# Bidirectional encoder layer on Trainium2: how the first RMSNorm gets its weight row at the beginning

## What is computed

```python
x = x + 0.5 * swiglu(rmsnorm(x, norm_ffn1), w_gate, w_up, w_down)      # D_FF = 2816
x = x + hybrid_mixer(rmsnorm(x, norm_mix), ...)                        # windowed attention and gated linear attention
x = x + 0.5 * swiglu(rmsnorm(x, norm_ffn2), ...)
y = rmsnorm(x, norm_final)

def rmsnorm(x, gain):
    return x * rsqrt(mean(x * x, axis=-1) + EPS) * gain
```

## Time and profile before

| | |
|---|---|
| median of three runs | 2169.91 us (2168.96 to 2171.39) |
| profiled execution, from first to last instruction | 2169.4 us; no time around it is given, the runs' median is 0.5 us longer |
| TensorE matmuls busy | 2138.6 us (99%) |
| VectorE busy | 1499.5 us (69%) |
| ScalarE busy | 842.6 us (39%) |
| GpSimd busy | 330.1 us (15%) |
| mean granted TensorE clock | 0.998 |
| the loads of x and of the weight row at the beginning, from issue to landing | 3.9 to 9.4 us, median 7.0 us |

### The profile page before, as it was taken

One profiled execution on the slowest core, in us unless ns is written; L12 is line 12 of the kernel. 1 busy time (PEld: TensorE's weight loads), 2 busy tenths in 40 slices (PEclk: granted clock), 3 DMA queues, 4 the chain that ended last, 5 costly groups with the idle time before them and its releaser, 6 DMA issues.

```text
span 2169.4 us, 32769 instructions
## 1 busy us (share of the span) xinstructions
PE 2138.6 (99%) x11956; PEld 1921.3 (89%) x11956; DVE 1499.5 (69%) x2704; ACT 842.6 (39%) x1688; POOL 330.1 (15%) x324
## 2 busy tenths in 40 slices
PE   6999999999999999999999999999999999999998
PEld 6999999999988888888888888899999999988887
DVE  7766677676666686988754556777777667757676
ACT  7333222222343355755543334422323322333343
POOL 7111111111100002201002344211111111100000
PEclk9999999999999999999999999999999999999999
DMA  4322222332586566433355972222322222387554
GB/s 128 101 82 91 92 88 88 97 101 97 176 292 211 174 208 171 126 111 94 94 149 170 292 229 101 65 94 92 115 82 82 92 91 88 113 291 257 174 186 166
DMA packets 245987, 301.17 MB, mean 139 GB/s; under 512 B 24194, under 2 KB 159746, under 8 KB 245828
## 3 DMA queue, kind: packets, MB, share of 16 engines
q1 hardware_dynamic: 237188, 285.97, 41.2%
q10 hardware_dynamic: 8640, 13.11, 1.7%
HBM read 206.29 MB, written 88.47 MB: 136 GB/s over the span
## 4 chain that ended last, share of the span: by engine, by line
PE 95%; DVE 2%; POOL 1%; DMA 1%; issue 1%; ACT 1%; SPq 0%; ACTq 0%; POOLq 0%; DVEq 0%
PE ps L2485 16%; PE ps L2481 12%; PE ps L2483 10%; PE ps L2484 10%; PE ps L2493 8%; PE ps L2495 8%; PE ps L2494 8%; PE ps L2408 4%; PE ps L2410 4%; PE ps L2409 4%; PE ps L2426 2%; PE ps L2428 2%; PE ps L2427 2%; PE ps L2680 1%; PE ps L2654 1%; POOL hs L1121 1%
## 5 line engine op out<-in xcount | busy, mean ns | idle before, releaser
L2485 PE MATMUL ps<-hs,w_lo 128*128 128x384 f32 (+1 forms) x992 | 305.0, 307 | 0.0
L2493 PE MATMUL ps<-w_hi,dh 128*128 128x512 f32 x770 | 300.2, 390 | 0.0
L2495 PE MATMUL ps<-w_hi,dh 128*128 128x512 f32 x770 | 299.7, 389 | 0.0
L1959 DVE TENSOR_TENSOR dh<-dr,dh 128x640 fp32r<-128x640 f32 x154 | 127.2, 826 | 161.4 <-ACT dh L1357 161.2
L2494 PE MATMUL ps<-w_lo,dh 128*128 128x512 f32 x610 | 237.3, 389 | 0.0
L2483 PE MATMUL ps<-hs,w_hi 128*128 128x384 f32 (+1 forms) x644 | 214.4, 333 | 3.4 <-DVE hs L1802 2.6
L1357 ACT CAST dh<-dr 128x640 fp32r<-128x640 f32 x154 | 112.2, 729 | 269.9 <-PE ps L2495 250.1
L2484 PE MATMUL ps<-hs,w_hi 128*128 128x384 f32 (+1 forms) x644 | 213.9, 332 | 0.0
L2481 PE MATMUL ps<-hs,w_hi 128*128 128x512 f32 x588 | 210.2, 391 | 0.0
L2481 PE MATMUL ps<-hs_first,w_hi 128*128 128x512 f32 x588 | 210.2, 391 | 0.0
L2484 PE MATMUL ps<-hq,w_hi 128*128 128x384 f32 x616 | 205.8, 334 | 0.0
(11 more groups left out here) (321 smaller groups left out, 4826.2 us busy)
## 6 DMA issues: line engine op xcount, KB each, us to landing
dr<-hid_mid SPq DMA_DIRECT2D x154, 320.0 KB, 3.2
w_raw<-in_w_ffn_down SPq DMA_DIRECT2D x176, 256.0 KB, 3.6
hid_mid<-st SPq DMA_DIRECT2D x88, 320.0 KB, 4.3
w_raw<-in_w_ffn_gate SPq DMA_DIRECT2D x44, 512.0 KB, 4.1
w_raw<-in_w_ffn_up SPq DMA_DIRECT2D x44, 512.0 KB, 3.9
hid_mid<-sg SPq DMA_DIRECT2D x66, 320.0 KB, 2.2
hq<-o_mid SPq DMA_DIRECT2D x70, 128.0 KB, 3.6
w_raw<-in_w_in SPq DMA_DIRECT2D x14, 512.0 KB, 5.4
```

Source lines behind the costliest of these rows:

```text
L1959: v.tensor_tensor(a_lo, DR[f][n % D_HID][:, :], a_hi.bitcast(F32), ALU.subtract).then_inc(W["a_lo"], 1)
L2485: last = mm(out, lo[:, k, :], b_hi, start=False, stop=k == 3, skip_group_check=True)
L2493: mm(out, hi, w_h, start=first and p in D_FRESH, stop=False, skip_group_check=True)
L2495: return mm(out, lo, w_h, start=False, stop=last, skip_group_check=True)
```

## The change

The weight row's load and the identity's leave SP's queue. ScalarE's queue issues both at its very beginning, ahead of the first square, and the weight row is now written to all 128 partitions of `gain_first` by one DMA (512 KB written). The two spreading matmuls, their wait and their mark are gone; VectorE waits for `gain_loaded` and reads the row from SBUF.

```diff
@@ -353,8 +353,6 @@
         def x_first(t):
             return piece(*X_SLOT[t])
 
-        GAIN_BANK = 2
-
         def xs_first(n):
             return piece(4, 3 + n % 4)
 
@@ -465,7 +463,7 @@
         gain_loaded = sem("gain_loaded")
         expo_set = sem("expo_set")
         pe_marks = sem("pe_marks")
-        GAIN_SPREAD, OUT_EARLY = 1, 2
+        OUT_EARLY = 1
 
         def named(prefix, names):
             return {k: sem(f"{prefix}_{k}") for k in names.split()}
@@ -742,9 +740,7 @@
                 sp.dma_start(to, g.to_broadcast([P, D_MODEL])).then_inc(gain_loaded, 16)
 
             load_x(0)
-            sp.dma_start(gain_first[0:1, :, :], norm_ffn1.rearrange("a (h n) -> a h n", h=2)).then_inc(gain_loaded, 16)
             load_x(5)
-            sp.dma_start(ident[:, :], c_ident).then_inc(ident_loaded, 16)
             load_x(1)
             load_x(6)
             load_gu(0, 0)
@@ -1396,6 +1392,8 @@
                         elif s + D_LEAD + 1 >= G_STEPS:
                             d_hi(f, s + D_LEAD + 1 - G_STEPS)
 
+            act.dma_start(gain_first, norm_ffn1.rearrange("a (h n) -> a h n", h=2).to_broadcast([P, 2, HALF])).then_inc(gain_loaded, 16)
+            act.dma_start(ident[:, :], c_ident).then_inc(ident_loaded, 16)
             norm_squares(0, 0)
             norm_squares(0, 1)
             for i in range(HT):
@@ -1776,10 +1774,10 @@
                     dve.wait_ge(x_spilled[n % 2], 16 * (HT + n // 2 + 1))
                     gain = gain2[:, :].rearrange("p (h n) -> p h n", h=2)
                 else:
-                    dve.wait_ge(pe_marks, GAIN_SPREAD)
+                    dve.wait_ge(gain_loaded, 16)
                     if n >= 4:
                         dve.wait_ge(N["turned"], 4 * (n // 2 - 1))
-                    gain = ps[:, GAIN_BANK:GAIN_BANK + 2, :]
+                    gain = gain_first
                 v.scalar_tensor_tensor(out=xs_norm(f, n), in0=x_norm(f, t), scalar=rstd[:, 2 * f, t:t + 1], in1=gain,
                                        op0=ALU.mult, op1=ALU.mult).then_inc(N["scaled"], 1)
 
@@ -2535,11 +2533,6 @@
                 last.then_inc(W["tile"], 1)
 
             pe.wait_ge(const_set, ONES)
-            pe.wait_ge(gain_loaded, 16)
-            for half in range(2):
-                last = mm(ps[:, GAIN_BANK + half, :], ones[0:1, 0:1].to_broadcast([1, P]), gain_first[0:1, half, :],
-                          start=True, stop=True)
-            last.then_inc(pe_marks, 1)
             pe.wait_ge(ident_loaded, 16)
             for i in range(3):
                 norm_turn(0, i)
```

## The result

The changed kernel takes 2176.82 us (median of seven runs, 2176.54 to 2177.32) against 2169.85 us of the kernel before, timed beside it (seven runs): 7.0 us longer, ratio 1.0032, 95% interval 1.0022 to 1.0042. The profiled execution spans 2175.5 us, 6.1 us more than that of before.

A forecast was written before the change was run, and what follows sets the result against it. The start was taken as the bound: a chain over loads of x, VectorE and GpSimd before TensorE's dense work. 1.1 + 1.2 + 1.8 + 0.1 + 0.3 = +4.5 us on 2169.91 gave 2174.4 us, range 2170.6 to 2177.6.

The forecast's parts named there:

- my case: Main forecast: SBUF operand makes VectorE and GpSimd exclude each other at the start; +4.5 us, own range +2.9 to +6.0.
- rival 2: Whole holds: six meetings each cost a whole operation, landing moves 1.35 us in full; +6.5 us, 2176.4 us; chance 0.16.
- The landing: Loads of x at the start: broadcast's extra bytes make the sixth tile land later, +0.65 us, lower end -1.35.
- Scalings 1 to 4: First norm's start: second and third scalings hold back GpSimd's ssq and roots, first block at 15.1 us; +1.1 us.
- The pair at 18.34: Scalings before the second block: second's ssq and root wait, one subtraction slips in ahead; +1.2 us.
- The pair at 26.56: Scalings running into four subtractions: one ahead of the second scaling, another ahead of the low part, 0.9 us each; +1.8 us.
- The last pair and the clock: Pair at 37.16, behind the products' start, covered by VectorE's idle time, +0.1 us; TensorE's lower clock level, +0.3 us.
- The signs: Expected in the trace: first product at 38 to 39 us, sixth tile's square 17.4 to 18.7, four subtractions near 6 us.
- Rival 1: Not slower: exclusion falls beside the path at the start, only the landing is left, +0.65 us, 2170.6 us; chance 0.15.
- Rival 3: A late broadcast: landing after 10.2 us, each further microsecond paid again; at 12 us +6.3, 2176.2 us; chance 0.04.

The follow-up runs named there:

- experiment 10: Kernel before with only the queue changed: ScalarE issues the 4 KB row and identity, TensorE still spreads the row; 2168.91 us, second set 2168.86 us.
- Experiment 1: Kernel before with the changed kernel's loads (512 KB broadcast and identity on ScalarE's queue), row still spread by TensorE and read from PSUM; 2169.47 us, ratio 0.9998.
- Experiment 2: Kernel before with the changed kernel's loads and TensorE's spread kept; first four scalings read the row from SBUF, other six from PSUM; 2172.21 us, ratio 1.0010.
- experiment 5: Kernel before plus ScalarE's copy of the spread row into SBUF, read there only by the seventh and eighth scaling; 2173.76 us, ratio 1.0017.
- experiment 8: Kernel before with the changed kernel's loads, TensorE's spread kept; all scalings read SBUF except seventh and eighth, which read PSUM; 2174.16 us, ratio 1.0020.
- experiment 9: Kernel before with the changed kernel's loads, TensorE's spread kept; all scalings read SBUF except ninth and tenth, which read PSUM; 2175.21 us, ratio 1.0026.
- experiment 6: Kernel before plus ScalarE's copy of the spread row into SBUF, read there only by the ninth and tenth scaling; 2171.96 us, ratio 1.0009.

## Why the prediction was right, and where it was not

The direction and the mechanism held: 2176.82 us lies in the range (2170.6 to 2177.6), above the 2174.4 us forecast and above my case's own range, which ended at +6.0 us. That it lies in the range is in part luck: the upper end came from rival 2, and neither its six meetings at the whole price nor its landing in full are what happened. By its steps, with block 0, 1, 2 and the product as marks:

- **The landing, +0.65 us.** Wrong by its size. The sixth tile landed where it had (17.33 us), for the queues moved 340 GB/s from 2 to 10 us; before it was 284. Half of the difference comes with the earlier issues alone (312 GB/s in experiment 10's second set, where the sixth tile's square starts at 16.95 us): by these traces, what the issues gave, some 0.4 us, the broadcast took. What I had not worked out is the first tile: its square starts at 6.92 to 6.95 us in every trace with the broadcast and at 4.43 to 4.64 without. That the two share the bandwidth is my reading. Experiment 1 shows that by itself this costs nothing that can be measured.

```profile
2.00:10.00 8.00, 0.00 (x0) 0.00 (x0) 0.87 (x1) 3.64 (x6) 1.21 (x3) 1.00 1.01 340
```

- **Scalings 1 to 4, +1.1 us; measured +3.3.** This is the term that failed. I let the second scaling start at its old time and counted two delayed roots. With the first tile late, the first scaling ran from 9.13 us and held the second tile's ssq (0.93 us) as well, so that all three roots waited: a chain of scaling, ssq, root of 2.01 us a turn, 3 x 2.01 = 6.0 us from the first scaling to the fourth, where before it was 4.4. And the fourth met GpSimd's sum of weights at 15.08 us (2.28 for 1.28 us), an operation that I had not put in its way. The later first scaling is 0.7 of the 3.3 us, the chain 1.6 and that meeting 1.0. Experiment 2: +2.7 us in the time. No kernel has these scalings from SBUF and the first tile at its old time, so how much of the chain goes back to the late tile is not shown.
- **The pair at 18.34, +1.2 us; measured +0.9** at block 1, by another road: since VectorE was later, both roots were ready, and the pair met one subtraction, the low part another.
- **The pair at 26.56, +1.8 us; measured +1.0.** I counted two new meetings and kept the two old ones, five operations against four subtractions of which one had already run. The two new ones are right, at 2.05 us together (experiments 5 and 8); what I had missed is that VectorE, being late, is spared one of the others (1.1 us).
- **The last pair and the clock, +0.1 and +0.3 us; measured +0.9** from the product to the end (2135.9 us after, 2135.0 before), of which 0.4 by the end of the last transposes. The sum is near and its parts are not. In the last pair the cover failed: it took 4.32 us, made TensorE wait 1.42 us and costs 1.6 to 2.25 us by the medians (experiments 9 and 6). My cover, VectorE's idle 1.30 us at 40.92, was a wait for TensorE at its lower clock level; the two traces of experiment 10 show that without that stretch there is none. The clock gave the difference back in the profiled executions: the 16 transposes behind the first product took 1.91 us where they had taken 2.97. The low level had fallen ahead of the products (0.50 from 28.0 to 34.3 us, full behind it), where TensorE had time to spare. I had taken the stretch in the products as paid already; it is paid in the one profiled execution, and most timed runs of the kernel before are of the shorter group. Against experiment 1, which has no such stretch either, it is 2.7 us from the product to the end (2135.9 for 2133.2).
- **The signs.** The first product at 39.60 us came behind the 38 to 39 that I had named, the sixth tile's square at 17.33 a little ahead of the 17.4 to 18.7. Four subtractions took up to 7.5 us and not 6. The first three scalings kept their 1.28 us, since beside the tiny ssq it is GpSimd that waits; the longer ones are the fourth and one in each of the next two pairs.

Rival 1 (only the landing, +0.65) is refuted: the fourth scaling and all three pairs took longer, and experiment 1 has the landing at nothing. Rival 3 (a late broadcast) too: it landed in 4.7 us, at 5.4 us. Rival 2 had the price of a meeting nearer than I: 1.0 to 1.1 us on VectorE, where I had taken 0.9. The Trainium skill, SBUF — State Buffer, section SBUF: two separate sides, has the lock held for the whole instruction; the ssq that ends 0.06 us behind a scaling of 1.28 us agrees with that. Rival 2's other half, the landing in full, did not show: the sixth tile came no later than before, and 0.4 to 0.7 us later than in experiment 10. The Trainium skill, DMA: Bandwidth & Descriptors, section Issuing engines are not separate DMA queues, gives a second issuer the sequencer's time back and no more. That the landing must then move by the whole 1.35 us was my conclusion, and it left out the gaps that earlier issues and the broadcast fill.

## What to carry to other kernels

Where VectorE and GpSimd both work on the critical path, look at which of VectorE's operands lie in SBUF: an operation with one of its two in PSUM runs beside GpSimd, the same one with both in SBUF takes turns with it, about 1 us per meeting here for both engines. Two matmuls that put a row into PSUM can thus be cheaper than a transfer that is free. Count meetings by walking both instruction lists in time, tiny operations included, since a chain that goes back and forth between the engines pays in each turn. An engine that comes later meets others, or none, so the costs of single edits need not add; and before medians that differ by 1 or 2 us are compared, look where the low clock fell.

## What the runs showed of the hardware that I had not expected

- A tiny operation of GpSimd (0.19 us) waited for the end of a scaling of VectorE three times in a row, up to 1.29 us each: a small one waits as long as a large one.
- The two engines take strict turns when both have work ready: 1.76, 1.75 and 1.75 us in a row for operations of 0.68 us, each behind one subtraction.
- 512 KB more at the start, from a second queue and with the other loads issued earlier, moved the sixth tile by nothing and the first by 2.3 us.
- A stretch of some 3 us at the lower clock level in the first products costs 1.8 us, and whether it is there differs between executions of the same kernel (2168.4 and 2167.0 us). The fourth pair's 16 transposes take 2.97 us with it and 1.91 without; the first pairs' take 3.65 to 3.68 us at a granted clock of 1.00 as well (9.89 and 17.15 us before), so their length is not the clock's.
